# Input projection of a two-layer decoder trunk: six column chunks in place of seven, turns of query and key tiles moved

## What is computed

```python
for l in range(DEPTH):                                   # 2 layers
    proj = jnp.einsum('btd,dn->btn', x, w_in[l])         # 1024 -> 2578
    (qa, ka, va, u, qc, kcm, vcm, ksl, vsl, kwi, vwi, gc) = jnp.split(proj, offsets, axis=-1)
    qa = apply_rope(...); ka = apply_rope(...)           # 384 columns each
    o_a = diff_attention(qa..., ka..., va, lam, ...)
    o_b = pool_mixer(u, w_pool[l], pool_scale[l])
    qc = apply_rope(...); kcm = apply_rope(...); ksl = ...; kwi = ...
    gates = jax.nn.sigmoid(gc)
    o_c = nsa_attention(qc, kcm, vcm, ksl, vsl, kwi, vwi, gates, ...)
    mix = concatenate([o_a, o_b, o_c]) @ w_out[l]
    x = layer_norm(ALPHA * x + mix, ...)
    x = layer_norm(ALPHA * x + jnp.square(relu(x @ w_up[l])) @ w_down[l], ...)
```

## Time and profile before

| | |
|---|---|
| median of three runs | 1256.25 us |
| profiled execution | 1256.2 us, of it the span 1254.4 us |
| PE busy | 1235.6 us (98%) |
| DVE, ACT, POOL busy | 725.2, 477.3, 488.9 us (58%, 38%, 39%) |
| granted TensorE clock, mean | 0.999 |

### The profile page before, as it was taken

One profiled execution on the slowest core, in us unless ns is written; L12 is line 12 of the kernel. 1 busy time (PEld: TensorE's weight loads), 2 busy tenths in 40 slices (PEclk: granted clock), 3 DMA queues, 4 the chain that ended last, 5 costly groups with the idle time before them and its releaser, 6 DMA issues.

```text
span 1254.4 us, 18654 instructions
## 1 busy us (share of the span) xinstructions
PE 1235.6 (98%) x7514; PEld 1026.6 (82%) x7514; DVE 725.2 (58%) x1120; ACT 477.3 (38%) x946; POOL 488.9 (39%) x277
## 2 busy tenths in 40 slices
PE   8999999999999999999999999999999999999997
PEld 8998666789888888888899976668988888888885
DVE  4396778369672262360397867783797623605406
ACT  5326678623222231222143366784333322222210
POOL 1468000044444444444345760003264444444442
PEclk9999999999999999999999999999999999999999
DMA  7533001132522322232224320013233332233211
GB/s 254 134 75 102 2 1 52 51 106 97 172 91 95 101 101 94 92 101 97 63 59 128 94 69 1 19 35 106 79 135 100 101 101 91 95 101 101 93 59 67
DMA packets 77973, 110.28 MB, mean 88 GB/s; under 512 B 17664, under 2 KB 38336, under 8 KB 77760
## 3 DMA queue, kind: packets, MB, share of 16 engines
q1 hardware_dynamic: 76304, 104.31, 26.4%
q10 hardware_dynamic: 1584, 4.78, 1.1%
HBM read 106.98 MB, written 2.10 MB: 87 GB/s over the span
## 4 chain that ended last, share of the span: by engine, by line
PE 91%; DVE 4%; ACT 2%; issue 1%; POOL 1%; DMA 0%; DVEq 0%; ACTq 0%; POOLq 0%
PE ps L683 17%; PE ps L685 16%; PE ps L684 16%; PE ps L679 9%; PE ps L680 9%; PE ps L681 9%; PE ps L788 3%; PE ps L776 2%; PE ps L825 2%; PE ps L638 1%; PE ps L810 1%; ACT probs_a L1169 1%; DVE negmax L1432 1%; DVE probs_a L1485 1%; PE ps L901 1%
## 5 line engine op out<-in xcount | busy, mean ns | idle before, releaser
L549 POOL TENSOR_TENSOR w_lo<-raw,w_hi 128x1024 fp32r<-128x1024 f32 (+3 forms) x182 | 420.9, 2319 | 645.2 <-ACT w_hi L1041 644.7
L1041 ACT ACTIVATE w_hi<-raw 128x1024 fp32r<-128x1024 f32 (+3 forms) x200 | 198.6, 995 | 593.2 <-PE ps L685 361.9
L679 PE MATMUL ps<-xt_hi,w_lo 128*128 128x512 f32 (+1 forms) x576 | 210.7, 366 | 0.0
L680 PE MATMUL ps<-xt_hi,w_hi 128*128 128x512 f32 (+1 forms) x576 | 210.5, 366 | 0.0
L681 PE MATMUL ps<-xt_lo,w_hi 128*128 128x512 f32 (+1 forms) x576 | 210.5, 365 | 0.0
L683 PE MATMUL ps<-w_hi,xt_lo 128*128 128x384 f32 (+3 forms) x448 | 152.5, 340 | 0.6 <-DVE xt_lo L1277 0.3
L683 PE MATMUL ps<-w_hi,mt_lo 128*128 128x512 f32 x384 | 150.5, 392 | 0.2
L684 PE MATMUL ps<-w_hi,mt_hi 128*128 128x512 f32 x384 | 149.5, 389 | 0.0
L685 PE MATMUL ps<-w_lo,mt_hi 128*128 128x512 f32 x384 | 149.4, 389 | 0.0
L685 PE MATMUL ps<-w_lo,xt_hi 128*128 128x384 f32 (+3 forms) x448 | 148.0, 330 | 0.0
L684 PE MATMUL ps<-w_hi,xt_hi 128*128 128x384 f32 (+3 forms) x448 | 148.0, 330 | 0.0
(11 more groups left out here) (175 smaller groups left out, 1865.8 us busy)
## 6 DMA issues: line engine op xcount, KB each, us to landing
raw<-in_w_up SPq DMA_DIRECT2D x64, 512.0 KB, 3.4
raw<-in_w_down SPq DMA_DIRECT2D x64, 512.0 KB, 3.8
raw<-in_w_in SPq DMA_DIRECT2D x32, 384.0 KB, 3.2
raw<-in_w_in SPq DMA_DIRECT2D x16, 256.0 KB, 2.8
raw<-in_w_in SPq DMA_DIRECT2D x32, 128.0 KB, 2.5
raw<-in_w_out SPq DMA_DIRECT2D x8, 512.0 KB, 3.2
raw<-in_w_out SPq DMA_DIRECT2D x12, 256.0 KB, 3.7
rows<-in_ln_g ACTq DMA_DIRECT2D x4, 512.0 KB, 3.9
```

The source lines that it names most:

```text
L549: nc.gpsimd.tensor_tensor(unit_of(w_lo, u), unit_of(raw, u), unit_of(w_hi, u).bitcast(F32), ALU.subtract).then_inc(s_lo_ready, 1)
L679: mm(o, wl[:, c], a_hi[:, k, cols], start=first, stop=False)
L680: mm(o, wh[:, c], a_hi[:, k, cols], start=False, stop=False)
L1041: A(unit_of(w_hi, u), unit_of(raw, u), ACT.Copy).then_inc(s_hi_ready, 1)
```

## The change

The chunks of the input projection are cut anew: six of 384, 384, 512, 402, 384 and 512 columns. Chunk 2 now holds KCM, VCM, KSL (384 columns in one piece) and KWI; chunk 3 holds QC and the gates; chunk 4 is the values of A, and is what chunk 5 was: by bank in its second half, with the first scores between. There are four units fewer in a layer (`U_LAST` is 20 instead of 24).

Chunk 4 uses the same banks as chunk 3 (`IN_BANK`), so it may start only when all four banks of chunk 3 are copied, and ACT now copies these in one go when chunk 3 has ended. The turns are split in three: KCM and VCM in the middle of chunk 3 (waiting for `roped_m` and the copies of chunk 2), four tiles between chunk 3 and chunk 4, two in the middle of chunk 4 (waiting for DVE's first two copies). The order of the work on DVE and on POOL is as before, by the new numbers of units: `rows_to_compress(1)` now stands behind `w_lo` 17 and `rows_to_compress(0)` behind `w_lo` 19. The exponentials of lambda move on ACT from n == 18 of 24 to n == 18 of 20.

```diff
-TURN_EARLY = ((12, 4), (6, 5), (0, 6), (3, 7)), ((1, 0), (4, 1), (2, 2), (5, 3))
+TURN_EARLY = (12, 0), (6, 1), (0, 2), (3, 3), (1, 0), (4, 1), (2, 2), (5, 3)
-IN_COLS = (((0, 384),), ((384, 384),), ((O_KCM, 256),), ((O_QC, 384),), ((O_VA, 384),), ((O_KSL, 128), (O_KWI, 128), (O_G, GATES)),
+IN_COLS = (((0, 384),), ((384, 384),), ((O_KCM, 384), (O_KWI, 128)), ((O_QC, 384), (O_G, GATES)), ((O_VA, 384),),
            ((O_U, 256), (O_VSL, 128), (O_VWI, 128)))
+IN_BANK = (0, 4, 0, 4, 4)
...
-            def turn_early(layer, n):
-
-                pe.wait_ge(s_roped_a, nth("roped_a", layer, TT))
-                if n == 0:
+            def turn_early(layer, first, end):
+
+                if first == 0:
                     pe.wait_ge(s_roped_m, nth("roped_m", layer, TT))
-                    pe.wait_ge(s_in_copied, nth("in_copied", layer, 4 * TT))
+                    pe.wait_ge(s_in_copied, nth("in_copied", layer, 3 * TT))
+                elif first == 2:
+                    pe.wait_ge(s_roped_a, nth("roped_a", layer, TT))
+                    pe.wait_ge(s_turned_act, nth("turned_act", layer, 2))
                 else:
-                    pe.wait_ge(s_in_copied, nth("in_copied", layer, 5 * TT))
-                for q, bank in TURN_EARLY[n]:
+                    pe.wait_ge(s_turned_dve, nth("turned_dve", layer, 2))
+                for q, bank in TURN_EARLY[first:end]:
...
                     if k == LAST - 1:
-
-                        pe.wait_ge(s_turned_act, nth("turned_act", layer, 2))
-                        pe.wait_ge(s_turned_dve, nth("turned_dve", layer, 2))
+                        turn_early(layer, 2, 6)
+                        pe.wait_ge(s_in_copied, nth("in_copied", layer, TT * k))
...
-                        gemm(layer, s, 4 * (k % 2), xt_hi, xt_lo, lambda kt: None, by_bank=2 if k == LAST - 1 else 0,
-                             halfway=(lambda: turn_early(layer, k - 4)) if k >= 4 else turn_parameters if k == 1 else None,
+                        halves = {LAST - 2: (0, 2), LAST - 1: (6, 8)}
+                        gemm(layer, s, IN_BANK[k], xt_hi, xt_lo, lambda kt: None, by_bank=2 if k == LAST - 1 else 0,
+                             halfway=(lambda: turn_early(layer, *halves[k])) if k in halves else turn_parameters if k == 1 else None,
...
+                    if n == U_LAST - 4:
+                        act.wait_ge(s_unit_used, nth("unit_used", layer, n))
+                        for b in range(TT):
+                            copy_in(layer, n // 4 - 1, b)
                     split_to(layer, n + RING)
-                    if n == 18:
+                    if n == 14:
                         copy_early(layer, 0)
                         copy_early(layer, 1)
+                    if n == 18:
                         act.wait_ge(s_lam_dot, nth("lam_dot", layer, 1))
                         A(lams[:, 2:4], lams[:, 0:2], ACT.Exp).then_inc(s_lam_exp, 1)
-                    if n >= 4 and n % 4 < 2:
+                    if 4 <= n < U_LAST - 4 and n % 4 < 2:
```

More of the change, by code:

```diff
@@ L591, in rope_k @@
                 def rope_k(tt):
-                    pool.wait_ge(s_in_copied, nth("in_copied", layer, TT * (LAST - 1) + tt + 1))
+                    pool.wait_ge(s_in_copied, nth("in_copied", layer, TT * 2 + tt + 1))
                     rotate(nc.gpsimd.tensor_tensor, link, tt, ((T_KSL, 4, 64, R_CCK, R_SCK),)).then_inc(s_roped_k, 1)
@@ L1068, in copy_in @@
             def copy_in(layer, k, b):
-                bank = LAST_BANK if k == LAST else 4 * (k % 2) + b
+                bank = LAST_BANK if k == LAST else IN_BANK[k] + b
                 at_ = 0
@@ L1096, in copy_early @@
                 act.wait_ge(s_turned, nth("turned", layer, n + 1))
-                q, bank = TURN_EARLY[n // 4][n % 4]
+                q, bank = TURN_EARLY[n]
                 to = ka[:, q - Q_KA, :] if q < Q_VCM else kvcm[:, 0 if q == Q_KCM else 1, :]
```

## The result

The changed kernel takes 1280.3 us (median of 4 runs, 1279.5 to 1281.7) against 1256.1 for the kernel before: a ratio of 1.0195, with a 95% interval of 1.0183 to 1.0206, so 24.2 us slower. The forecast was 1277, with 1266 to 1286 as its range. The profiled execution took 1281.7 us, its span is 1279.9. Its first load came 0.6 us later than before (6.7 against 6.1); subtract that when times of layer 0 are laid beside those of before.

A forecast was written before the change was run, and what follows sets the result against it. PE was taken as the bound, gapless through the input projection. Per layer, waits of 4.6 + 0.5 + 7.6 less gains of 1.4 and 1.0 gave +10.3 us, twice +20.6: 1277 us, range 1266 to 1286.

The forecast's parts named there:

- The gain: Input projection: 96 fewer matmuls a layer save 1.4 us; shorter PE waits for ACT's `pt_a` save 1.0 a layer.
- the sum: Per layer, 12.7 us of waits less 1.4 and 1.0 of gain: +10.3; twice, +20.6.
- Stall A: Middle of chunk 3: PE waits 4.6 us for DVE's second rotary step before turning KCM; bounds 2.3 to 6.2.
- Stall B: Between chunks 3 and 4: PE waits 0.5 us for ACT's four copies of the same banks; bounds 0.2 to 1.0.
- Stalls C and D: PE waits for DVE's QC rotation and copies: 3.7 us mid chunk 4, 3.9 before first scores; 0 to 9.5 together.
- Clock: Rival, chance 0.15: PE's clock falls in the stalls; C's fall is hidden, A's and D's cost 10.8 us more, 1288.
- likeliest case: Main forecast, chance 0.60: the summed waits and gains with no clock fall, 1277 us, within 1271 to 1282.
- Not slower: Rival, chance 0.06: DVE runs nearly unheld, C and D are nothing; +0.1 to +0.4 us a layer, 1257.
- Milder company: Rival, chance 0.13: DVE and POOL interleave better, half the holds of C and D vanish; 5.6 us a layer, 1267.

The follow-up runs named there:

- half first step: Changed kernel with the rotary step of QA and KA done for two row tiles of four: 1280.5 us, ratio 1.0198.
- copies in one go: Changed kernel with ScalarE copying chunk 2's four banks together when chunk 3 begins, instead of two then and two a unit later: 1278.5 us, ratio 1.0178.

## Why the prediction was right, and where it was off

**The gain.** The distances were 0.227 us for 512 columns and 0.184 for 402, where I had 0.1809 from the slope: 0.3 us a layer less gain. The waits for `pt_a` shrank by 1.4 us over both layers where I took 2.0. The kernel with the rotations left out and lambda early shows what is left: 2.8 us in all, against 3.8 in the sum (its own waits for `pt_a` shrank by 1.1).

**Stall A** was 4.2 us against 4.6, with the mechanism that the prediction gave: DVE started on QA at 54.07 - 0.6 = 53.5 (said 53.46), ended at 73.2 - 0.6 = 72.6 (said 72.6), started on KCM behind the copies and ended at 80.9 (said 81.0). The half first step and the copies in one go bear out that the copies of chunk 2 set the start.

**Stall B** was 0.5, as said.

**Stalls C and D** were 3.6 and 2.1 (said 3.7 and 3.9). DVE started on QC at 96.12 - 0.6 = 95.5 instead of 93.0: that is the low clock behind A, handed on. It took to 113.2 through lambda, 17.1 us against 17.7. D is shorter for that, and because PE, at the low clock, came 1.4 us later. The kernel without the additions and the one that holds `w_lo` 20 and 21 back show both neighbours at work.

**The clock** was the term that the sum lacked. The prediction had it as a rival with 0.15, with falls in A and D that count and one in C that is hidden, 10.8 us. It fell in A and C in both layers; A's counted 2.6 each, C's was hidden, D's did not come. By layer the sum then reads 4.2 + 0.5 + 3.6 + 2.1 of waits, 2.6 and 1.4 of low clock, less 1.9 of gain (2.8 / 2 from the kernel with the rotations left out, and the 0.5 of B that is still in it): 12.5, twice 25.0. The spans differ by 1279.9 - 1254.4 = 25.5, of it 0.6 the later first load, so 24.9; the medians by 24.2. The rival *Clock* and the likeliest case should not have been kept apart: waits of 4 us on PE were the forecast's own product, and the only rows on an idle PE did not say that less than 5 us is harmless. Within A, a wait of 4.2 us, the clock fell.

**How much of it was luck.** The waits, 10.4 us a layer against 12.7 in the sum, are the mechanism that was forecast, and 1.4 of the 2.3 that they are short moved from waiting to work at the low clock. The low clock on the path, 5.2 us of the 24.2, was not in the sum, and nothing in the prediction held it down to that: its own rival had 10.8, and 1288 is outside the range. D brought no fall; with the rival's 2.7 a layer for it the time would have come to the range's upper end.

**The rivals.** *Not slower* is excluded for this order of chunks: PE waits for DVE in both places. It did come true where DVE's steps were left out or put in another order. *Milder company* did not happen: every `w_lo` that met one of DVE's rotary steps held it.

## What to carry to other kernels

Saving fixed cost per matmul shortens the engine that is the bound, and with it the time in which all others have done their part; before a chunk is cut away, list what is due at each point where the bound engine reads another's result, and move those dates too. Here a gain of 2.8 us came with 24 us of loss, and 1.9 us of gain were left once the longest step on DVE was fed first and one `w_lo` moved. Look also at what comes after the point you mend: twice the POOL steps that no longer stood in the way before the first scores stood in the way behind them.

## What the runs showed of the hardware

A DVE step with two inputs in SBUF waits for a running POOL step however small it is: two steps of one column took 1.87 and 2.27 us instead of 0.16 each beside `w_lo` of 2.4 us, while copies from PSUM (L1415, 0.69 us) ran beside POOL unchanged. The Trainium skill ("SBUF — State Buffer", "Who interferes with whom") says that a DVE instruction with two SBUF inputs contends with a GpSimd instruction that reads SBUF, and one with at most one SBUF input does not (outside DVE's 2-port modes); the rows agree.

PE's clock fell to 0.50 within waits of 3.2 to 4.2 us (less one matmul's distance) or just behind them, at most 1.1 us after PE had gone on, and in the kernel without the additions on KCM 0.8 and 1.0 us behind waits of 2.1 us. It stayed at 1.00 through one wait of 3.6 us whose like in the other layer lowered it, and through stall D of the changed kernel (2.1 us). Once down in the input projection, it was down for 3.4 or for 6.8 us, over PE's next work: in the changed kernel from 80.3 to 87.2. Its cost showed only where PE did not have to wait for another engine next.
